# Storing the transposed expert table in whole 4 KB rows: units of four panels, one per quarter of the partitions

## The reference, cut to what matters

```python
idx = jnp.take_along_axis(cidx, pos, axis=-1)
gates = jax.nn.softmax(best, axis=-1)
...
ue = jnp.take(u, it, axis=0)
act = jax.nn.gelu(jnp.einsum('tkd,td->tk', ue, ht), approximate=False)
ve = jnp.take(v, it, axis=0)
return jnp.einsum('tk,tkd->td', gt * act, ve)
```

## Time and profile before

| | us |
|---|---|
| median of 3 runs | 2452.68 (2451.73 to 2464.09) |
| the profiled execution, its own time | 2467.93 |
| its span, first to last instruction | 2465.9 |
| PE busy in the span | 2088.7 (85%) |
| DVE busy | 1563.3 (63%) |
| POOL busy | 829.3 (34%) |
| ACT busy | 482.5 (20%) |

### The profile page before, as it was taken

The page is one execution under the profiler, slowest core; times in us unless marked ns, Lnnn a source line. Parts: engine busy times, 40 slices in busy tenths (PEclk is TensorE's granted clock), DMA queues, the critical chain, the costliest instruction groups (busy, mean ns, idle before and its releaser), DMA issues. The chain is left out here.

```text
span 2465.9 us, 24437 instructions
## 1 busy us (share of the span) xinstructions
PE 2088.7 (85%) x8036; PEld 1398.4 (57%) x8036; DVE 1563.3 (63%) x3423; ACT 482.5 (20%) x1053; POOL 829.3 (34%) x637
## 2 busy tenths in 40 slices
PE   5998759866979898999998888888866669989977
PEld 3865748755835895555555555555422257724445
DVE  4458554445999985666666666666777776336752
ACT  3344022212211330000000000000000221334541
POOL 2420014423301004665555445544566232300002
PEclk8988569988989999999999999999988879989999
DMA  5988868994956459999999999999999421100001
GB/s 196 342 271 222 232 208 296 327 284 166 281 177 238 168 191 382 403 403 403 403 402 402 402 402 402 402 403 404 402 401 402 165 90 62 52 22 1 1 35 68
DMA packets 253069, 648.10 MB, mean 263 GB/s; under 512 B 20752, under 2 KB 119184, under 8 KB 251536
## 3 DMA queue, kind: packets, MB, share of 16 engines
q1 hardware_dynamic: 167552, 335.60, 39.6%
q0 software_dynamic: 73728, 268.47, 27.6%
q10 hardware_dynamic: 11664, 42.47, 5.1%
HBM read 560.48 MB, written 85.98 MB: 262 GB/s over the span
## 5 line engine op out<-in xcount | busy, mean ns | idle before, releaser
L1514 PE MATMUL ps<-arena 128*128 128x512 f32 x1024 | 513.9, 649 | 145.5 <-DVE arena L1371 108.0
L1382 DVE CUSTOM_DVE_ANT_0 arena<-arena 128x1024 bf16<-128x1024 f32 x256 | 313.4, 1225 | 254.8 <-DMA arena<-u_rows,expert 144.4
L1503 PE MATMUL ps<-rows_n,arena 128*128 128x256 f32 x2048 | 464.4, 379 | 0.0
L1503 PEld LDWEIGHTS ps<-rows_n,arena 128*128 128x128 f32 x2048 | 386.6, 190 | 95.4 <-issue 49.5
L1514 PEld LDWEIGHTS ps<-arena 128*128 128x128 f32 x1024 | 205.9, 207 | 399.3 <-issue 255.9
L1253 POOL DMA_INDIRECT arena<-u_rows,expert x256 | 284.8, 1112 | 313.9 <-DMA gates<-arena 171.2
L1253 POOL DMA_INDIRECT arena<-in_v,expert x192 | 207.0, 1078 | 328.2 <-DVE arena L1403 303.8
L199 DVE STREAM_TRANSPOSE tdst<-tsrc 128x1024 f32<-128x1024 f32 x128 | 153.6, 1226 | 163.6 <-DMA tsrc<-in_u 162.9
L1403 DVE SCALAR_TENSOR_TENSOR arena<-arena,wt 128x1024 f32<-128x1024 f32 x192 | 246.2, 1282 | 0.4
L1480 ACT ACTIVATE ge<-dots 128x2 f32<-128x2 f32 x128 | 26.0, 203 | 912.2 <-DVE dots L1382 912.2
L243 POOL TENSOR_TENSOR in_wlo<-in_raw,in_whi 128x1024 fp32r<-128x1024 f32 x45 | 115.7, 2573 | 236.1 <-ACT in_whi L239 236.1
(11 more groups left out here) (383 smaller groups left out, 3015.0 us busy)
## 6 DMA issues: line engine op xcount, KB each, us to landing
tsrc<-in_u SPq DMA_DIRECT2D x64, 1024.0 KB, 9.3
u_rows<-tdst SPq DMA_DIRECT2D x256, 256.0 KB, 5.4
arena<-in_u SPq DMA_DIRECT2D x128, 512.0 KB, 10.6
arena<-in_v SPq DMA_DIRECT2D x128, 512.0 KB, 11.5
in_raw<-in_panels ACTq DMA_DIRECT2D x37, 512.0 KB, 3.8
gates<-arena SPq DMA_DIRECT2D x8, 2048.0 KB, 8.7
arena<-gates SPq DMA_DIRECT2D x32, 512.0 KB, 18.7
mg_raw<-in_panels ACTq DMA_DIRECT2D x28, 512.0 KB, 6.4
```

The source lines that it names most:

```text
L1382: nc.vector.tensor_tensor_reduce(out=junk[:, n % 2], in0=u_slot[n % NU], in1=hrows[:, n // NPICK], scale=1.0, scalar=0.0, op0=ALU.mult, op ...
L1503: mm = nc.tensor.matmul(ps[:, j % 2, 0:TD], ud[:, j % RJ, k], rows_n2[:, 0, k], start=k == 0, stop=k == KD - 1)
L1514: mm = nc.tensor.matmul(ps[:, 4 + 2 * t + c], park[:, j % NPK, t * P:(t + 1) * P], vd[:, j % RJ, c * T:(c + 1) * T], start=j == 0, stop=j ...
```

## The change

A unit is now four panels. Panel a of the four goes to quarter a of the partitions of `tsrc`, with the four quarters of the model dimension side by side there: four loads of 512 KB, each to 32 partitions in pieces of 4 KB. A turn takes block column b of all four panels at once. Its result has whole rows: partition 32a + l holds the 1024 values of expert 32b + l of panel a. So a turn is stored by one transfer of 512 KB from 128 partitions, in pieces of 4 KB. The rows of a unit of four panels stand in another order, so that two bits of the row number trade places with two others; five small integer instructions make the row numbers `u_row` from the experts' numbers. `tdst` holds two single turns in place of two units of two. The next load is issued after every fourth turn, for the unit two ahead. To make room for the larger `tsrc`, `hq` takes the buffer of `hf`, and `prob` is cut to the width used. In `mg` the turns are spread evenly over 38 places, in place of three at each fourth one.

```diff
         def load(self, sp):
-            j, n = self.n_load, len(self.src) * self.unit
-            if j - self.first >= n:
-                sp.wait_ge(self.turned, j - n + self.unit)
-            k = (j - self.first) // self.unit % len(self.src)
-            sp.dma_start(self.src[k], io["u"][j:j + self.unit].rearrange("j p k e -> p j k e")).then_inc(self.loaded[k], 16)
-            self.n_load += self.unit
+            n = self.n_load
+            if n >= 2:
+                sp.wait_ge(self.turned, 4 * (n - 1))
+            for a in range(4):
+                sp.dma_start(tsrc[32 * a:32 * a + 32, n % 2],
+                             io["u"][4 * n + a].rearrange("(q l) k e -> l q (k e)", q=4)).then_inc(self.loaded[n % 2], 16)
+            self.n_load += 1
...
         def after(self, sp):
-            j = self.n_store
-            k = (j - self.first) // self.unit % len(self.dst)
-            sp.wait_ge(self.turned, j + self.unit)
-            rows = u_rows[j * EXP_N:(j + self.unit) * EXP_N]
-            for q in range(4):
-                sp.dma_start(rows[:, q * 256:(q + 1) * 256].rearrange("(b l) d -> l b d", l=32),
-                             self.dst[k][32 * q:32 * q + 32].rearrange("l j b k d -> l (j b) (k d)")).then_inc(self.stored[k], 16)
-            self.stores[k] += 1
-            self.n_store += self.unit
-            if self.n_load < self.end:
+            x = self.n_store
+            sp.wait_ge(self.turned, x + 1)
+            sp.dma_start(u_rows[P * x:P * x + P], tdst[:, x % 2]).then_inc(self.stored[x % 2], 16)
+            self.n_store += 1
+            if x % 4 == 3 and 4 * self.n_load < EXP_N:
                 self.load(sp)
...
         def turn(self, v):
...
+            x = self.n_turn
+            n, b = divmod(x, 4)
+            if b == 0:
+                v.wait_ge(self.loaded[n % 2], 64 * (n // 2 + 1))
+            if x >= 2:
+                v.wait_ge(self.stored[x % 2], 16 * (x // 2))
+            blocks = tsrc[:, n % 2].rearrange("p q (k b l) -> p (q k) b l", k=KD, b=4)
+            nc.vector.transpose(tdst[:, x % 2].rearrange("p (x l) -> p x l", l=32), blocks[:, :, b]).then_inc(self.turned, 1)
             self.n_turn += 1
...
-    tsrc = sbr(turn_st, "tsrc", [P, 2, 2, KD, P])
-    tdst = sbr(turn_st, "tdst", [P, 2, 2, 4, KD, 32])
+    tsrc = sbr(turn_st, "tsrc", [P, 2, 4, KD * P])
+    tdst = sbr(turn_st, "tdst", [P, 2, D])
...
-        places = [4 * m for m in range(KD) for x in range(3)] + [4 * KD + m for m in range(KD - 2)]
-        panel_stage("mg", PAN["merge"], with_side(specs, lambda u, s: sum(turns_after(x, range(len(places)), T_MG)
-                                                                          for x, y in enumerate(places) if y == u)),
-                    weights=mg_weights)
+        mms = list(range(5 * KD - 2))
+        panel_stage("mg", PAN["merge"], with_side(specs, lambda u, s: turns_after(u, mms, T_MG)), weights=mg_weights)
...
-                    nc.vector.scalar_tensor_tensor(out=expert[:, t - ND], in0=ptile[:, x % 2, 1], scalar=float(EXP_N), in1=ptile[:, x % 2, 0],
-                                                   op0=ALU.mult, op1=ALU.add).then_inc(S["expert"], 1)
+                    e, (swap_a, swap_b) = expert[:, t - ND], (u_row[:, NG + a] for a in range(2))
+                    step(nc.vector.scalar_tensor_tensor(out=e, in0=ptile[:, x % 2, 1], scalar=float(EXP_N), in1=ptile[:, x % 2, 0],
+                                                        op0=ALU.mult, op1=ALU.add))
+
+                    nc.vector.tensor_scalar(swap_a, e, 2, 0x60, ALU.logical_shift_right, ALU.bitwise_and)
+                    nc.vector.tensor_scalar(swap_b, e, 2, 0x180, ALU.logical_shift_left, ALU.bitwise_and)
+                    step(nc.vector.tensor_scalar(u_row[:, t - ND], e, 0x3e1f, None, ALU.bitwise_and))
+                    step(nc.vector.tensor_tensor(swap_a, swap_a, swap_b, ALU.bitwise_or))
+                    nc.vector.tensor_tensor(u_row[:, t - ND], u_row[:, t - ND], swap_a, ALU.bitwise_or).then_inc(S["expert"], 1)
```

More of the change, by code:

```diff
@@ L148, in __init__ @@
         def __init__(self):
-            self.loaded = [top.enter_context(nc.semaphore(f"tn_loaded{k}")) for k in range(3)]
-            self.stored = [top.enter_context(nc.semaphore(f"tn_stored{k}")) for k in range(3)]
+            self.loaded = [top.enter_context(nc.semaphore(f"tn_loaded{k}")) for k in range(2)]
+            self.stored = [top.enter_context(nc.semaphore(f"tn_stored{k}")) for k in range(2)]
             self.turned = top.enter_context(nc.semaphore("tn_turned"))
             self.n_load, self.n_turn, self.n_store = 0, 0, 0
-            self.loads, self.stores, self.filled = [0] * 3, [0] * 3, [0] * 3
@@ L168, in fill @@
         def fill(self, sp):
-            while self.n_load < min(self.end, self.first + len(self.src) * self.unit):
+            while self.n_load < 2:
                 self.load(sp)
         def after(self, sp):
-            j = self.n_store
-            k = (j - self.first) // self.unit % len(self.dst)
-            sp.wait_ge(self.turned, j + self.unit)
-            rows = u_rows[j * EXP_N:(j + self.unit) * EXP_N]
-            for q in range(4):
-                sp.dma_start(rows[:, q * 256:(q + 1) * 256].rearrange("(b l) d -> l b d", l=32),
-                             self.dst[k][32 * q:32 * q + 32].rearrange("l j b k d -> l (j b) (k d)")).then_inc(self.stored[k], 16)
@@ L180, in after @@
-            self.stores[k] += 1
-            self.n_store += self.unit
-            if self.n_load < self.end:
+            x = self.n_store
[3 more added lines that the diff above has]
+            if x % 4 == 3 and 4 * self.n_load < EXP_N:
                 self.load(sp)
         def drain(self, sp):
-            for k in range(3):
-                if self.stores[k]:
-                    sp.wait_ge(self.stored[k], 64 * self.stores[k])
+            for k in range(2):
+                sp.wait_ge(self.stored[k], 16 * (EXP_N // 2))
@@ L203, in program @@
     turn_st = ExitStack()
-    tsrc = sbr(turn_st, "tsrc", [P, 2, 2, KD, P])
-    tdst = sbr(turn_st, "tdst", [P, 2, 2, 4, KD, 32])
+    tsrc = sbr(turn_st, "tsrc", [P, 2, 4, KD * P])
+    tdst = sbr(turn_st, "tdst", [P, 2, D])
     T_IN, T_WA, T_HG, T_MG, T_N2, T_PQ = TURNS
     assert T_IN + T_WA + T_HG + T_MG + T_N2 + T_PQ == EXP_N
-    turner.begin([tsrc[:, k] for k in range(2)], [tdst[:, k] for k in range(2)], 2, EXP_N)
     with ExitStack() as st:
@@ L284, in _ @@
                         also(sp)
-                    for x in range(turns // turner.unit):
+                    for x in range(turns):
                         turner.after(sp)
@@ L402, in _ @@
                     side_load(sp)
-                for x in range(sum(s["kind"] == "U" for s in specs) // turner.unit):
+                for x in range(sum(s["kind"] == "U" for s in specs)):
                     turner.after(sp)
@@ L482, in attention_stage @@
         with ExitStack() as st:
-            prob = sb(st, name + "_prob", [P, NPB, T])
+            prob = sb(st, name + "_prob", [P, NPB, max(j["n"] for j in jobs)])
             ptT = sb(st, name + "_ptT", [P, 2, chunks, T])
@@ L630, in program @@
     b1h = ExitStack()
-    hf = sb(b1h, "hf", [P, HG, T])
+    hq = hf = sb(b1h, "hq", [P, HG, T])
     hg = sb(b1h, "hg", [P, HG, T])
@@ L826, in _ @@
         def _(sp):
-            for x in range(T_HG // turner.unit):
+            for x in range(T_HG):
                 turner.after(sp)
@@ L1032, in program @@
     expert = sb(pr, "expert", [P, NG, NPICK], U32)
+    u_row = sb(pr, "u_row", [P, NG + 2, NPICK], U32)
     gate = sb(pr, "gate", [P, NT, HEADS, TOPK])
@@ L1250, in _, with fetch @@
         def _(pool):
-            def fetch(dst, table, n, landed):
+            def fetch(dst, table, rows, n, landed):
                 t, k = divmod(n, NPICK)
@@ L1254, in fetch @@
                     out=dst, out_offset=None, in_=table,
-                    in_offset=bass.IndirectOffsetOnAxis(ap=expert[:, t, k:k + 1], axis=0)).then_inc(landed, 16)
+                    in_offset=bass.IndirectOffsetOnAxis(ap=rows[:, t, k:k + 1], axis=0)).then_inc(landed, 16)
             def fetch_u(n):
```

9 lines of the change are left out of this document (2 added, 7 removed).

## The result

The changed kernel takes 2536.57 us (median of 4 runs, 2531.67 to 2540.66) where the kernel before took 2458.39 beside it: a ratio of 1.0315, 95% interval 1.0286 to 1.0343, some 78 us slower. The forecast was slower by 30 us, 2483 with a range from 2430 to 2512, so the time lies above the range.

The account below looks back on a forecast made before the run. PE was taken to bound `in1`, VectorE `wa`, transfers the recurrence and `mg`; 2.3 (`in1`) + 3 (`wa`) + 9.6 (recurrence) + 11.2 (`mg`) + 2.8 (index arithmetic) + 1 (`n2`, `pq`) = +29.9 us on 2452.7 gave 2483, range 2430 to 2512.

Parts of the forecast that it names:

- The mechanism: Turn stages: loads to 32 partitions run at 209 GB/s, and a unit's third turn waits for its first's store behind them.
- The recurrence's cycle: Recurrence: 18.5 us from one unit's last turn to the next's, four cycles, stage +9.6 us.
- the slow begin: Start of a load block right after stores: 2 us at 78 in place of 209 GB/s, priced at 1.25 us.
- load and panels together 10.5 us: Stages with panels on ACT's queue: panels fill part of the idle half, block without slow begin 10.5 us, cycle 17.8.
- two turns were priced at 2.4 us: End of each cycle of four turns: the last two turns take 2.4 us together.
- index arithmetic: Row numbers: five instructions of 0.275 us and their chain, 1.4 us for two groups of tokens, +2.8 us, from 0 to 3.
- The upper end of the cycle, 19.8: Slowest cycle where panels run, load and panels at 12.5 us; with it `in1` would lose 14.3 us.
- the slack of the softmax chain: `wa`: takes up half of 2 us of waiting in each of three cycles, stage +3 us, from 0 to +7.
- Even spreading in `mg`: `mg`: VectorE's own work falls between third and fourth turn at times, 0.7 us on average, cycle 18.5 us, stage +11.2.
- The faster one: Rival: 32 partitions do not slow a load, or engines drift apart; -25 us, 2427 us, chance 0.28.
- The third: Rival, slower by much: full half speed everywhere, cycles at their upper ends; +67 us, 2520 us, chance 0.15.
- The fourth: Rival: whole-row stores from 128 partitions go no faster than today's, 2.5 us each, 2.4 more per cycle; no own chance.

Follow-up runs that it names:

- Experiment 1: The changed kernel with its four loads of a unit each to all 128 partitions; 2451.1 us, 0.9974 of the kernel before.
- experiment 2: The changed kernel with one quarter of a unit's load behind each turn's store, in place of all four behind every fourth; 2486.54 us, 1.0115.
- thin panels: The changed kernel with each weight panel after a stage's first four loaded to an eighth, 2496.16 us; the same in the kernel before, 2460.57 us.
- Experiment 5: The changed kernel with the turns of `mg` at the places of the kernel before; 2527.85 us, 1.0265 of the kernel before.

## Why the prediction was right in its sign and wrong in its size

**The mechanism** was the one that came: the half rate passed from stores to loads (206 GB/s, taken as 209), T2 waits for a store behind the block of loads, and transfers in the turn stages set the pace. Experiment 1 shows the first. The second is in the trace: in all 18 cycles of `in1`, the recurrence and `mg`, T2 starts 0.02 us after the landing of S0, and experiment 2 shows that another order in the queue gives 50 us back. The Trainium skill's rule on 32 partitions (SBUF — State Buffer, "Door 1: The DMA port swizzle"), which the rows before had shown for stores only, agrees for loads: its 189 GB/s for such a range, with transfers of 1 MiB, stands beside 206 here, with 512 KB each, and 357 for the same loads to 128 partitions.

The cycle can be taken apart by the issues and landings of its transfers and the times of its turns: S3 from issue to landing; the block, from there to the landing of the last of the four loads; S0, from there to its own landing; and from T2's start to T3's end. Means in us, from one T3's end to the next over the same cycles as in the prediction (six, four and eight):

| | S3 | block | S0 | T2 to T3 | sum |
|---|---|---|---|---|---|
| recurrence, forecast | 3.55 | 11.25 | 1.3 | 2.4 | 18.5 |
| recurrence, changed kernel | 3.2 | 11.0 | 1.2 | 2.5 | 17.9 |
| in1, forecast | 3.55 | 10.5 | 1.3 | 2.4 | 17.8 |
| in1, changed kernel | 3.6 | 12.7 | 1.7 | 3.7 | 21.7 |
| in1, thin panels | 3.1 | 11.3 | 1.3 | 3.3 | 19.0 |
| mg, forecast | 3.55 | 10.5 | 1.3 | 3.1 | 18.5 |
| mg, changed kernel | 3.9 | 12.2 | 1.8 | 3.6 | 21.5 |
| mg, thin panels | 3.1 | 11.3 | 1.3 | 3.2 | 19.0 |

**The recurrence's cycle** was summed to 18.5 us and is 18.0; the load's 10.0 us and the slow begin, together 11.25, measured 11.0. The stage lost 3.0 us where 9.6 were forecast: from its begin to the end of its last turn it is 6.6 us longer (84.3 against 77.7; the four cycles took 71.7 us in place of 74.0), and some 3.5 more are gone because the stage of before went on for 6.6 us behind its last turn and this one for 3.1.

**The step that failed** is the term "load and panels together 10.5 us" in `in1` and `mg`, and with it the reason given, that panels "fill part of the idle half". It measured 12.7 us in `in1` and 12.2 in `mg`. The term had left out the slow begin of 1.25 us, and with thin panels the block still takes 11.3; the panels add 1.4 and 0.9. They also lengthen the stores around it, and with them the wait for S1 between T2 and T3: in all, thin panels take 2.7 us off the cycle of `in1` and 2.5 off that of `mg`. In the stretch shown, in the first blocks of `in1`, it is worst: 2.1 MB of loads at 149 GB/s are 14 us, and those two blocks took 14.4 and 14.2. The cycles came to 21.7 and 21.5 us against 17.8 and 18.5.

A second, smaller step is the end of the cycle in `in1`: two turns were priced at 2.4 us, and from T2's start to T3's end it is 3.7. Half of the difference is VectorE's own work between them, which the prediction had counted in `mg` only (0.7 us, as measured there); the other half is T3 waiting for S1.

Six cycles at 3.9 us more are 23 us: the 28th turn of `in1` ended at 181.8 where I had 158.4, and the stage lost 22.3 us in place of 2.3. Eight cycles at 3 us more and a first unit 5 us later than worked out are 29 us: `mg` lost 41.0 in place of 11.2. The sum was short by 48 us: 20 from `in1`, 30 from `mg`, 6 from `wa` and 1 from `pq`, less 7 from the recurrence and less the index arithmetic that can't be seen. Of the 50 us in `in1` and `mg`, thin panels give back 35.

The upper end of the cycle, 19.8, had the block at 12.5 us, which is about what came; the other 2 us over it are the slower stores and the time between T2 and T3. That end cut the range at 2512.

**A wait priced at nothing.** With VectorE that late, PE waits for its copies in `in1`, from that stage's waits:

```profile
PE ps L655 <- DVE hg L457: 21.5, 2, 21.1
```

I had given VectorE's lateness no effect on PE inside `in1`. It changes no number, since VectorE's last turns set the end anyway, but it is how a stage bound by PE comes to be bound by a queue.

**`wa`** lost 9.3 us, forecast 3. VectorE's waits for stores there are 7.8 us in all, four of up to 2.7 us where three of 2 were worked out, and the slack of the softmax chain that was to take up half of them does not show in the stage's length.

**Index arithmetic.** The five added instructions take 219 to 292 ns each, two of each kind, about as forecast (275):

```profile
L1327 DVE TENSOR_TENSOR u_row<-u_row 128x128 uint32<-128x128 uint32 x2 | 0.6, 292 | 0.1
...
L1325 DVE TENSOR_SCALAR u_row<-expert 128x128 uint32<-128x128 uint32 x2 | 0.4, 219 | 0.0
```

From the start of ranking to the end of the span are 1747 us in the changed kernel and 1746 to 1761 in the kernels without the arithmetic, so its 2.8 us can't be seen in the whole.

**Even spreading in `mg`** was said to put VectorE's own work between T2 and T3. Experiment 5 gives back 12 us of `mg` for the old places, but through an earlier first unit, not a shorter cycle (T2's start to T3's end is 3.5 us there, against 3.6): right in sign, wrong in its reason.

**The rivals.** The faster one fell with the 206 GB/s. The third, slower by much, was the case that came, and past its price of 2520; I gave it 0.15. Its own test, the 28th turn of `in1` after 170, was met (181.8). The fourth fell: S0 takes 1.2 us behind the block in the recurrence, not 2.5.

## What to carry to other kernels

Here a transfer's rate went with the partitions it touches in SBUF, in both directions: 206 and 209 GB/s with 32, 357 and 351 with 128. A new layout that widens one of two transfers may narrow the other, so price both, and price other queues' traffic beside the narrow one as taken from it. When transfers share one queue, ask for each wait what stands ahead of the awaited transfer: a unit of work longer than its output buffers puts the next load between a store and the turn that needs it. Where a narrow transfer can't be avoided, try to interleave it with wide ones in the same queue: with the alternating order of the quarters that made the kernel before 1.2% faster, of which the order alone had given 0.6%.

## What the runs showed that was not expected

Weight panels beside a block of loads to 32 partitions do not use the other half of the rate: both together moved 229 GB/s with the engines full (the loads 149 of it, 220 with thin panels), and removing seven eighths of the panels' bytes took 16 us off `in1` and 20 off `mg`, against 6 in `mg` where the traffic was mixed. And the short store buffers, which looked like the second cause, cost nothing that can be told in units of two (1.0044 against 1.0046). The same loads at half rate cost 42 to 47 us in units of two and 85 in units of four.
